# Two blocks on one core: single tiles at the ends of the first block's stages, norm chains without steps between, own places for modulation pieces, a larger share for the context's mixer, and earlier top-16 work

## What is computed

```python
def first_block(x, c, ...):                    # latents only
    for l in range(2):
        mod = silu(c) @ w_ada[l] + b_ada[l]    # six rows: shift, scale, gate, twice
        h = rms_norm(x, g_pre_mix[l]) * (1 + sc_m) + sh_m
        y = token_mixer(h, w_in[l], ..., w_out[l])      # 1024 -> 3656, attention, 1024 -> 1024
        x = x + gt_m * rms_norm(y, g_post_mix[l])
        h = rms_norm(x, g_pre_ffn[l]) * (1 + sc_f) + sh_f
        y = conv_glu_ffn(h, ...)               # up to 2 x 2816, conv, gelu, down to 1024
        x = x + gt_f * rms_norm(y, g_post_ffn[l])

def second_block(x, c, ctx, c_ctx, ...):
    # layer 0: even_mixer (context attends to itself, latents to both), then peer for both
    # layer 1: odd_mixer, then peer for the latents only
def peer(h, w_q, subkeys, u, v):               # per token: 8 heads x 16 experts of 16384
    s = (h @ w_q) . subkeys; idx, g = top-16 pairs
    return sum_k g_k * gelu(h . u[idx_k]) * v[idx_k]
```

## Time and profile before

| | |
|---|---|
| median of 3 executions | 3838.68 us (3829.47 to 3843.15) |
| profiled execution, its own time | 3842.15 us |
| its span in the trace | 3840.9 us |
| PE busy | 3050.1 us, 79% |
| DVE busy | 2455.0 us, 64% |
| ACT busy | 784.2 us, 20% |
| POOL busy | 940.7 us, 24% |
| granted TensorE clock | 0.909 of full speed |
| HBM read | 1099.18 MB, 286 GB/s over the span |
| gathers of expert rows, software queue | 818.87 MB |

### The profile page before, as it was taken

How to read it: one execution, slowest core, us unless ns; L and a number is a source line. 1 busy time by engine, 2 the same in 40 slices (tenths; PEclk the granted TensorE clock), 3 DMA queues, 4 the chain that set the end, 5 groups by cost and what they waited for, 6 DMA issues and landing times. The chain is left out here.

```text
span 3840.9 us, 28366 instructions
## 1 busy us (share of the span) xinstructions
PE 3050.1 (79%) x8769; PEld 1590.1 (41%) x8769; DVE 2455.0 (64%) x5374; ACT 784.2 (20%) x1876; POOL 940.7 (24%) x842
## 2 busy tenths in 40 slices
PE   6898797899786799787767777777897787777776
PEld 1354464675334377254344223322343462233322
DVE  3224556887677488646656999766514519999665
ACT  1102223232224433225211111100102211111000
POOL 0000001222221233222302344434100013444432
PEclk7999898999898899888879998999996799999999
DMA  6654234999795689966847999999632059999998
GB/s 236 201 178 167 93 114 169 343 356 354 301 356 199 230 349 406 373 248 212 306 154 294 391 388 389 392 422 422 257 138 103 21 206 367 386 389 376 422 421 348
DMA packets 194025, 1102.15 MB, mean 287 GB/s; under 512 B 22517, under 2 KB 22849, under 8 KB 95569
## 3 DMA queue, kind: packets, MB, share of 16 engines
q0 software_dynamic: 114512, 818.87, 54.1%
q1 hardware_dynamic: 78736, 280.90, 20.2%
q10 hardware_dynamic: 624, 0.57, 0.1%
HBM read 1099.18 MB, written 1.05 MB: 286 GB/s over the span
## 5 line engine op out<-in xcount | busy, mean ns | idle before, releaser
L2022 PE MATMUL PS<-AR 128*128 128x512 f32 x2464 | 1216.7, 639 | 400.7 <-DVE AR L2064 341.2
L2121 POOL DMA_INDIRECT AR<-in_uv,AR x768 | 866.1, 1128 | 1641.9 <-PE PS L2022 1142.8
L2069 DVE CUSTOM_DVE_ANT_0 AR<-AR 128x1024 f32<-128x1024 f32 x768 | 935.6, 1220 | 297.2 <-DMA AR<-in_uv,AR 296.7
L2022 PEld LDWEIGHTS PS<-AR 128*128 128x128 f32 x2464 | 476.1, 202 | 1103.3 <-DVE AR L2064 536.5
L694 PE MATMUL PS<-AR 128*128 128x512 f32 (+3 forms) x1304 | 565.3, 588 | 27.4 <-DMA AR<-in_w_in 14.7
L2034 ACT ACTIVATE AR<-AR 128x2 f32<-128x2 f32 x384 | 78.1, 203 | 1514.8 <-DVE AR L2069 1509.2
L694 PEld LDWEIGHTS PS<-AR 128*128 128x128 f32 x1304 | 250.5, 205 | 314.9 <-issue 269.5
L991 PE MATMUL PS<-AR 128*128 128x256 f32 x1408 | 327.2, 392 | 22.9 <-DMA AR<-in_w_up_act 11.9
L326 DVE SCALAR_TENSOR_TENSOR AR<-AR,CC 128x512 f32<-128x512 f32 x280 | 210.5, 752 | 208.5 <-DMA AR<-in_w_ada 130.7
L991 PEld LDWEIGHTS PS<-AR 128*128 128x128 f32 x1408 | 273.2, 196 | 85.0 <-issue 17.4
L1941 PE MATMUL PS<-AR 128*128 128x256 f32 x768 | 186.7, 406 | 26.7 <-DMA AR<-in_peer_w_q 19.6
(11 more groups left out here) (226 smaller groups left out, 2490.3 us busy)
## 6 DMA issues: line engine op xcount, KB each, us to landing
AR<-in_w_mod SPq DMA_DIRECT2D x96, 512.0 KB, 4.3
AR<-in_w_ada SPq DMA_DIRECT2D x96, 512.0 KB, 4.6
AR<-in_w_in SPq DMA_DIRECT2D x56, 512.0 KB, 4.0
AR<-in_peer_w_q SPq DMA_DIRECT2D x48, 512.0 KB, 3.3
AR<-in_w_up_act SPq DMA_DIRECT2D x44, 512.0 KB, 7.7
AR<-in_w_up_lin SPq DMA_DIRECT2D x44, 512.0 KB, 7.5
AR<-in_w_down SPq DMA_DIRECT2D x44, 512.0 KB, 9.6
AR<-in_even_w_in SPq DMA_DIRECT2D x24, 512.0 KB, 4.2
```

The costliest lines, as they stand in the source:

```text
L2022: ins = pe.eng.matmul(acc[i][hh], e.dg(x), e.buf(x)[:, 1024 + 512 * hh:1536 + 512 * hh], start=(x == e.on[False][i][0]), stop=(x == e.on[F ...
L2069: v.eng.tensor_tensor_reduce(e.buf(x)[:, 0:1024], e.buf(x)[:, 0:1024], norm2(e).H[e.tiles[x // 128]], 1.0, 0.0, ALU.mult, ALU.add, DT[x // ...
L2121: g.eng.indirect_dma_start(e.buf(x), None, D["uv"][e.l], bass.IndirectOffsetOnAxis(ap=idx_at(x // 16, x % 16, 1), axis=0)).then_inc(*land. ...
```

## The change

- `lin_pe` gets `whole`: for the columns named, all 4 chunks are held in the ring and tile 0 runs through all of them, then tile 1. It is used for the first 512 columns of w_in in layer 1 (`HEAD`), for the second 512 of w_out in layer 1 (`TAIL`), and for the first columns of w_in and the second 512 of w_out in the latents' even mixer. The last four chunks of `down` are done in the same way in both layers. In a held block of a stage's end, PE has nothing of its own in the first two of its four yields; at a stage's head, nothing in the last two.
- The norm chain goes tile by tile: `rms_y` per tile with the square-root table loaded first (`root_first`), `square` of x right behind it, `scale_dve` of tile 0 between the two tiles' `add_dve`, of tile 1 behind them. `yield 1.5` and `yield 2.0` are gone; the `yield 1.0` before `up` stands one place earlier on PE.
- The pieces of three modulation sets (both layers' `first`, layer 0's `next`) get seven places of 512 columns of their own; each piece is loaded and released in two halves of 0.25 MB. The first seven loads wait for the transposes of the norm before (`guard`). Layer 1 takes no piece beside its first four w_in chunks.
- PACE is 0.6, the ranges for the choice between PE and DVE are moved (`ATTENTION`, `UPDOWN`), and the context's gathers into slot 0 wait for all its score matmuls.
- For the latents' experts `begin` is 3 and `under` is 4; the set `more` sums in another area, and layer 0's gathers and top-16 don't wait for it.

```diff
+        OWN_T = [T[:, a:a + 512] for a in (1536, 3072, 3584)] + [HTt[:, 2048 + 512 * i:2560 + 512 * i] for i in range(4)]
+        OWN_BIG = [BIG[:, 5632 + 512 * i:6144 + 512 * i] for i in range(3)] + [T[:, 1024 + 512 * i:1536 + 512 * i] for i in range(4)]
...
                     for kh in range(4):
-                        load(sp, ("raw", self.key, j, hh, kh), self.w[r, kh].rearrange("p (c n) -> p c n", c=2),
-                             2, 512, [("piece", self.key, j, hh, kh)])
+                        if n:
+                            for c in range(2):
+                                i = self.nth(j, hh, kh, c) % n
+                                sp.wait_ge(place.get(i, self.guard))
+                                sp.eng.dma_start(self.own[i], self.w[r, kh, :, 512 * c:512 * c + 512]).then_inc(
+                                    *land.landed(f"own{i}", "raw", self.key, j, hh, kh, c))
+                                place[i] = ("piece", self.key, j, hh, kh, c)
...
+        def root_first(a):
+            a.wait_ge(a.last)
+            a.eng.activation(dum, dum, ACT.Sqrt).then_inc(*a.done())
...
+            def square(self, a, t):
+                ss, sq = sm(1, "nss", t), sm(1, "nsq", t)
+                a.wait_ge(a.last, self.xev[t])
+                a.eng.activation(self.H[t], Xt[:, t, :], ACT.Square, accum_out=ss).then_inc(*a.done())
+                a.wait_ge(a.last)
+                a.eng.activation(sq, ss, ACT.Sqrt, scale=1.0 / 1024, bias=eps).then_inc(*a.done("nsq", *self.key, t))
...
+                if c0 in whole:
+                    if k0 == 0:
+                        held = [(x, *chunk(pe, block(w, nk, c0, n, x, kk), kk, n, False)) for x in range(0, nk, kk)]
+                    i = k0 // kk - (0 if c0 == cols[0] else 2)
+                    if 0 <= i < 2:
+                        t = tiles[i]
+                        if t not in seen:
+                            prep.prep(pe, t)
+                            seen[t] = prep.turned(t)
+                        pe.wait_ge(seen.get(t))
+                        for x, k, wt in held:
+                            pe.wait_ge(("raw", k))
+                            for kc in range(kk):
+                                ins = pe.eng.matmul(bks[i][:, 0:n], lhs(x + kc, t), wt[:, kc, :],
+                                                    start=(x + kc == 0), stop=(x + kc == nk - 1))
...
-        CH, ROW, PACE, ATT = 0.45, 0.47, 0.8, (1.2, 0.5)
+        HEAD, TAIL = ((), (0,)), ((), (512,))
+        CH, ROW, PACE, ATT = 0.45, 0.47, 0.6, (1.2, 0.5)
...
+                if f == 18:
+                    held = [(x, *chunk(pe, wd[:, x:x + 1, :], 1, 1024, False)) for x in range(18, 22)]
+                for x, k, wt in held if f >= 20 else ():
+                    pe.wait_ge(("raw", k), ("glu", l, x))
+                    down(x, k, wt, f - 20)
...
         def add_dve(v, l, gate, key, mods):
             for t in range(2):
+                if t:
+                    after(l, gate).scale_dve(v, 0)
...
             v.events["added", l, gate] = v.last
+            after(l, gate).scale_dve(v, 1)
...
             def take(a, t, c0, n):
+                if c0 and t == 0:
+                    root_first(a)
                 take_y(a, ("lin", "wout", l), t, c0 // 512, ("mm", "lin", "wout", l, t, c0))
+                if c0:
+                    rms_y(a, l, 2, t)
+                    n2.square(a, t)
 
             for _ in lin(a, 8, (0, 1024), [0, 1], take):
                 yield CH
-            rms_y(a, l, 2)
-            yield 1.5
-            n2.squares(a)
...
-        ATTENTION, UPDOWN = range(98, 112), range(124, 188)
+        ATTENTION, UPDOWN = range(108, 122), range(131, 195)
...
-                    g.wait_ge(("mm", "sco", e.key, 15 if e.halved and e.slot[x] == 5 else 0))
+                    g.wait_ge(("mm", "sco", e.key, 15 if e.halved and e.slot[x] in (0, 5) else 0))
...
         of_lat = [Experts(f"l{l}", l, [0, 1], LAT, 3, MAIN, HTt[:, 0:1024], WIDE, 0, 3, MAIN,
-                          mods.finished() + [("sum", before, 255)], 11, 1)
-                  for l, mods, before in ((0, more, "c"), (1, mods_of["odd"], "l0"))]
+                          [("sum", before, 255)] + mods, 3, 4)
+                  for l, mods, before in ((0, [], "c"), (1, mods_of["odd"].finished(), "l0"))]
```

More of the change, by code:

```diff
@@ L249, in next_chunk, with chunk @@
             sp.used += 1
-        def chunk(pe, src, nk, nw):
+        def chunk(pe, src, nk, nw, wait=True):
             k = pe.used
@@ L646, in prep @@
                 elif lane.name == "dve":
-                    for x in self.fresh(t):
+                    for x in self.fresh(t) if not self.early else ():
                         self.scale_dve(lane, x)
@@ L675, in block, with lin_pe @@
             return w[at_:at_ + 128 * kk * n].rearrange("(p k n) -> p k n", k=kk, n=n)
-        def lin_pe(pe, key, w, nk, cols, tiles, lhs, prep=None, seen=None, ring=MAIN):
+        def lin_pe(pe, key, w, nk, cols, tiles, lhs, prep=None, seen=None, ring=MAIN, whole=()):
             seen = {} if seen is None else seen
+            held = []
             for t in tiles[0:1] if len(ring) > 3 else tiles:
@@ L905, in first_pe @@
             pe.run(mods_of["first", l])
-            for _ in lin_pe(pe, ("win", l), D["w_in"][l], 8, (0, 3656), [0, 1], LAT.tile, prep=n1, ring=FIRST[l]):
-                pe.fill()
+            for i, _ in enumerate(lin_pe(pe, ("win", l), D["w_in"][l], 8, (0, 3656), [0, 1], LAT.tile, prep=n1, ring=FIRST[l],
+                            whole=HEAD[l])):
+                if i >= 4 * len(HEAD[l]):
+                    pe.fill()
                 yield CH
@@ L972, in first_pe @@
                 seen[t] = turned_all(("om", l, t), 8)
-            for _ in lin_pe(pe, ("wout", l), D["w_out"][l], 8, (0, 1024), [0, 1], LAT.tile, seen=seen, ring=FIRST[l]):
+            for _ in lin_pe(pe, ("wout", l), D["w_out"][l], 8, (0, 1024), [0, 1], LAT.tile, seen=seen, ring=FIRST[l],
+                            whole=TAIL[l]):
                 yield CH
-            yield 1.5
             pe.run(mods_of["next", l])
@@ L1045, in first_pool @@
             g.run(mods_of["first", l])
-            for _ in lin(g, 8, (0, 3656), [0, 1], nothing, prep=n1):
-                g.fill()
+            for i, _ in enumerate(lin(g, 8, (0, 3656), [0, 1], nothing, prep=n1)):
+                if i >= 4 * len(HEAD[l]):
+                    g.fill()
                 yield CH
@@ L1197, in first_act @@
                     take_y(a, ("y", ("ffn", l)), t, hh, ("mm", "y", ("ffn", l), t))
-            rms_y(a, l, 3)
-            yield 2.0
+                rms_y(a, l, 3, t)
+                after(l, 3).square(a, t)
         def gelu_act(a, l, ft):
@@ L1449, in even_pe @@
             ring = RINGS[side]
-            for _ in lin_pe(pe, ("ein", side), W2, 8, (0, 416), tiles, lay.tile, prep=n1, ring=ring):
+            for _ in lin_pe(pe, ("ein", side), W2, 8, (0, 416), tiles, lay.tile, prep=n1, ring=ring,
+                            whole=(0,) if side == "l" else ()):
                 pe.fill(1, side)
@@ L1519, in even_pe @@
             for _ in lin_pe(pe, ("eout", side), D["even_w_out_2"][0], 8, (0, 1024), tiles,
-                            lambda kc, t: lay.tile(kc, t) if kc < 4 else b.CT[:, kc - 4, lay.cols(t)], seen=seen, ring=ring):
+                            lambda kc, t: lay.tile(kc, t) if kc < 4 else b.CT[:, kc - 4, lay.cols(t)], seen=seen, ring=ring,
+                            whole=(512,) if side == "l" else ()):
                 pe.fill(1, side)
@@ L1545, in even_act @@
             nk = len(keys)
-            if side == "l":
-                n1.squares(a)
             def take_pq(a, t, c0, n):
```

143 lines of the change are left out of this document (81 added, 62 removed).

## The result

| | before | after |
|---|---|---|
| median of 9 executions each, on the same chip | 3845.51 us | 3826.73 us (3819.94 to 3841.86) |
| ratio | | 0.9959, 95% interval 0.9939 to 0.9979 |
| profiled execution, its span | 3840.9 us | 3826.3 us |

The change makes the kernel 0.4% faster, 16 us. The forecast was 67 us less, 3775 us, and the time lies above the range given (3740 to 3815).

A forecast was written before the change was run, and what follows sets the result against it. Limits were taken as differing by stage (PE, DVE, DMA, or none), with work order limiting the chains between. Chains, held chunks, own places, guard, early part, tail and latents summed to -67: 3842 - 67 = 3775 us, range 3740 to 3815.

The forecast's parts named there:

- The early part: 100 to 654 us, w_in and attention of layer 0: moved mixer work and 14 expert steps cost 0, bounds -30 and +51.
- rival C: Mixer work lengthens w_in of layer 0, attention doesn't shorten, experts come on top: 3854 us, chance 0.07.
- Rival A: Early expert steps aren't hidden; DVE's order makes the first block's attention wait: +51, 3826 us, chance 0.12.
- Chains behind `down`: Norm chains after `down` of layers 0 and 1: tile order lets PE start sooner, -19 and -18 us.
- Chain behind w_out of layer 1: Norm chain ahead of `up`, which needs both tiles: 27 us becomes 12 to 13, -14.
- rival E: Chains keep their length as ACT or DVE come late from expert steps; half of 55 us lost: 3802, chance 0.12.
- Chain behind w_out of layer 0: Norm chain without held chunks, so tile 0 is ahead by only 1.7 us: -4 us.
- Held chunks: Four buffers wanted at once, so the last chunk loads later and PE may wait: +6 us, bounds 0 and 20.
- Own places: Ring left to the weights alone: -6 and -5 us, at w_in of layer 1 and `up` of layer 0.
- SP's guard wait: SP waits for transposes, delaying weight chunks at w_in and `up` of layer 0: +5 us, bounds 0 and 12.
- Rival B: DMA takes the chains' gain back, 15 steps' rows missed: +37, 3812 us, chance 0.10.
- Rival D: Early part evens out, `up` starts 30 us earlier beside the chains' gain: 3745 us, chance 0.09.

The follow-up runs named there:

- own_and_latents: Kernel before plus only the own places and the latents' part, without tile order, held chunks, removed yields and 0.6: 3823.85 us, 0.9958.
- pace80: Changed kernel with the context's mixer and queries counted at share 0.8 instead of 0.6, ranges moved to fit: 3854.6 us, 1.0019.
- held_experts: Changed kernel, share still 0.6, with the context's expert steps held back by 8.1 shares: 3875.42 us, one execution.
- yields_back: Changed kernel with the 1.5 and 2.0 yields put back ahead of the norms' transposes, tile order kept: 3835.07 us, 0.9984.
- no_own_places: Changed kernel with the three modulation sets' pieces back in the ring of four: 3854.14 us, 1.0016.
- latents_old: Changed kernel with the latents' experts as before the change: 3838.24 us, 0.9977.
- far_old_order: own_and_latents with the context's expert steps held back by 150 shares, until the main stream is through: 4273.19 us, one execution.
- far_tile_order: Changed kernel with share 0.8, the 1.5 and 2.0 yields back and the context's expert steps held back by 150 shares: 4226.10 us, one execution.

## Why the prediction was wrong, point by point

- **The early part, taken at 0, is the step that failed.** w_out of layer 0 ended at 632.2 and ends at 696.5: +64, beyond the upper bound of +51. Of the 66 us up to `up`, own_and_latents shows 2, pace80 7.5, and held_experts parts the other 58 into 30 and 28. The bound of 42 + 9 was for the expert steps alone, and they cost less than that, 28. The mixer's 28 us of work beside a full PE had no upper bound at all in my sum, since I credited attention with the same amount. The window showed the room (PE idle 41 us), not that work in the order of a chain could use it. This is rival C's mechanism: 66 us are lost before `up` starts, just over its 64. Its time, 3854, wasn't right: it has 28 + 51 = 79 us for the early part, and the expert steps cost 28, not 51; w_out of layer 0 ends 64 us later. The signs named for it are there: `up` starts at 719.8, not at 650 +/- 15, and w_in and attention are both longer.
- **Rival A** names the measured time, 3826, and that is luck. It has the expert steps cost 51 us; they cost 28, and the 30 us of the moved mixer and queries aren't in it. Of its mechanism, attention waiting in the order of the engines, the 28 us are what is shown.
- **Stretch behind it: right in its sum, in part by luck.** Chains, held chunks and own places behind w_out 0 were -55 + 6 - 11 = -60. From the end of w_out of layer 0 to the end of the even mixer it was 1255.4 us (632.2 to 1887.6) and is 1191.1: -64. Inside it the terms were off in both directions: the chains gave 52 us, all stages between them together 12.
- **Chains behind `down`** (-19, -18): -22.6 and -26.1 in the chains, with the tiles where they were forecast. The latents' even mixer behind the second is 254.0 us where it was 248.4, so about 20 of the 26 stay. But the reason I gave, the tile order, is half of it or less: with the steps in place (yields_back) the chains are still 26.3 us where they were 32.7, and 24.1 where they were 36.3. The rest is the 4.3 steps no longer there, which the tail pays. I had the tail's side in the sum, under the shares, and so the total came out.
- **Chain behind w_out of layer 1** (-14): -5. The tile 0 that should come 7 us early did not. ACT first ran a gelu of the context and then the table load:

```profile
1345.38 0.20 ACT L2110 ACTIVATE AR<-AR 128x2 f32<-128x2 f32 x1 [9.66 <-DVE AR L2145]
...
1345.61 1.28 ACT L624 ACT_TABLE_LOAD   x1
...
1347.13 0.60 ACT L1150 ACTIVATE AR<-PS 128x512 f32<-128x512 f32 x1
...
1366.27 3.62 PE L2098 MATMUL PS<-AR 128*128 128x512 f32 x4
```

  ACT takes up tile 0 at 1347.13, at the end of w_out and not ahead of it, and PE has an expert sum of 3.62 us before the first `up` matmul. This is rival E, in one chain; what of the 9 us missing is ACT's part and what the expert sum's is not shown. **Chain behind w_out of layer 0** (-4): +1.6.
- **Held chunks** (+6, bounds 0 and 20): `up` and `down` of layer 1 take 253.7 us for 250.9, +3, at 399 GB/s as forecast.
- **Own places** (-11) are a term mis-sized: -16.5 and -8.3 by no_own_places. The first lies outside the bound of -15, but the bound counted from the 160 us of the kernel before, and this counts from the 168.0 of the new order without places. Against the kernel before (own_and_latents) they are -9.7 and -6.8, inside the bounds and 5.5 more than forecast in sum. **SP's guard wait** (+5): none is seen at w_in of layer 0 in the changed kernel (335.0 us with it, 334.3 without); at 0.8 own_and_latents takes 291.9 us for it where the kernel before took 289.7.
- **Tail** (-6): 60.9 us to 56.1, -5. With the share at 0.8 it would have been 104, so the 17 steps were worth 48, as counted ahead of pace80 (46). The mistake was in what they cost at the other end.
- **Latents' experts** (-6): 7 by latents_old; in the trace of layer 0 the dot products are 2.67 us apart up to the 112th and 2.45 behind it, as forecast.
- **The table load.** The Trainium skill (ScalarE: Activation LUTs, What ACT_TABLE_LOAD costs) adds a drain of 1.38 us to the load. In the chain behind `down` of layer 0 the user starts at 1028.18, 0.01 us behind the load's end (1026.89 + 1.28), as in the earlier trace rows. Nor does a drain stand ahead of a load: the load at 1345.61 follows an instruction that ends at 1345.58. The trace doesn't agree, and no run shows the -5.5 us by that rule.
- **Rival B** found no support: `up` and `down` of layer 1 at the same rate are only 3 us longer. **Rival D** is refuted by the early part.

## What to carry to other kernels

An engine's idle share tells how much work a stage lacks, not that other work can use it: where two chains share every engine's order, their steps add up (7.4 + 8.9 us here), and moving work out of such a stage need not shorten it either (209 and 211 us). When work of a second stream stands in a chain, measure the chain without it (18.2 us, not 34.5) before crediting a new order with the difference. And buffers of their own for the side loads, with the latents' part, reach the whole change's time by themselves (0.9958 and 0.9959); what all the reordering and the share add can't be measured.

## What the runs showed that I had not expected

The granted clock behaved otherwise in the two kernels without expert steps. The attention part of the latents' even mixer, the same 268 matmuls, first far_old_order, then far_tile_order:

```profile
1523.70:1590.70 67.00, 58.34 (x268) 41.59 (x269) 30.73 (x78) 21.18 (x48) 0.00 (x0) 0.72 0.00 1
```

```profile
1494.80:1552.20 57.40, 47.48 (x268) 34.69 (x269) 30.75 (x78) 21.16 (x48) 0.00 (x0) 0.91 0.00 1
```

At a mean clock of 0.72 PE was busy for 58.3 us, at 0.91 for 47.5, with the same work of DVE and ACT. The clock was thus longer at the lower of its levels, 1.2 GHz, in the first: by the means 37.5 of 67.0 us, and 10.3 of 57.4. In the whole stretch PE's busy time fell from 864.1 to 839.5 us for 3122 matmuls, so at most 25 of the 36 us that the tile order won without steps are clock. Each is one execution, and the attention itself is alike in both, so whether the shorter chains ahead of it did this stays open. With expert steps beside it the clock of the stretch was 0.91 and 0.92, and nothing of the kind was there to win.
